# Norm boundaries of a two-part transformer stack: sums of squares in four column parts of TensorE, first products passed in another order

## The reference, cut to what matters

```python
x = x + gate * y
h = rms_norm(x, g) * (1 + scale) + shift
... h @ W ...

def _rmsnorm(x, g, eps=RMS_EPS):
    x32 = x.astype(jnp.float32)
    y = x32 * lax.rsqrt(jnp.mean(x32 * x32, axis=-1, keepdims=True) + eps)
    return (y * g.astype(jnp.float32)).astype(x.dtype)
```

## The kernel before

| boundary, start of Ln (us) | what follows | ahead | ada |
|---|---|---|---|
| 561.0, 1653.5 | MLP | two units | no |
| 927.2 | dilated attention, behind a barrier of all engines | no | 48 sums |
| 2019.6 | recurrent mixer | four quarters | 48 sums |
| 2752.7, 3343.0 | convolutional FFN | two units | no |
| 3135.0 | Fourier and convolution mixer | two units | 16 sums |
| 3722.7 | transposes and output | no | no |

## Time and profile before

### The profile page before, as it was taken

One profiled execution on the slowest core, in us unless ns is written; L12 is line 12 of the kernel. 1 busy time (PEld: TensorE's weight loads), 2 busy tenths in 40 slices (PEclk: granted clock), 3 DMA queues, 4 the chain that ended last, 5 costly groups with the idle time before them and its releaser, 6 DMA issues. The chain is left out here.

```text
span 3739.8 us, 62013 instructions
## 1 busy us (share of the span) xinstructions
PE 3428.5 (92%) x25014; PEld 2625.2 (70%) x25014; DVE 1960.2 (52%) x2407; ACT 1283.4 (34%) x2213; POOL 1168.0 (31%) x626
## 2 busy tenths in 40 slices
PE   6899989999899999789999997788699999989998
PEld 4445567888676777568888886666578877668876
DVE  8345536565355343556565573444357554853444
ACT  3245522223445455321223433332132223142222
POOL 0000024443565554134443322000035443124443
PEclk9899989999899999799999998788799999989999
DMA  6222214443343434225453211000035443113332
GB/s 243 82 79 68 65 62 173 158 169 112 113 133 113 128 112 110 93 78 186 152 175 98 76 54 40 4 4 4 25 124 185 140 161 99 56 62 96 95 95 79
DMA packets 261706, 383.85 MB, mean 103 GB/s; under 512 B 40406, under 2 KB 185466, under 8 KB 250234
## 3 DMA queue, kind: packets, MB, share of 16 engines
q1 hardware_dynamic: 257144, 366.90, 30.7%
q10 hardware_dynamic: 4354, 13.98, 0.9%
HBM read 360.90 MB, written 19.92 MB: 102 GB/s over the span
## 5 line engine op out<-in xcount | busy, mean ns | idle before, releaser
L487 POOL TENSOR_TENSOR w_lo<-w_raw,w_hi 128x1024 fp32r<-128x1024 f32 x302 | 750.4, 2485 | 1831.8 <-ACT w_hi L478 1831.8
L500 PE MATMUL ps<-h_hi,w_hi 128*128 128x512 f32 x2432 | 958.7, 394 | 66.9 <-DVE h_lo L684 33.2
L501 PE MATMUL ps<-h_hi,w_lo 128*128 128x512 f32 x2432 | 954.8, 393 | 0.0
L502 PE MATMUL ps<-h_lo,w_hi 128*128 128x512 f32 x2432 | 953.9, 392 | 0.0
L478 ACT ACTIVATE w_hi<-w_raw 128x1024 fp32r<-128x1024 f32 x302 | 320.3, 1061 | 1182.9 <-PE ps L502 1154.2
L500 PEld LDWEIGHTS ps<-h_hi,w_hi 128*128 128x128 f32 x2432 | 462.1, 190 | 179.2 <-issue 36.9
L502 PEld LDWEIGHTS ps<-h_lo,w_hi 128*128 128x128 f32 x2432 | 461.6, 190 | 97.1
L501 PEld LDWEIGHTS ps<-h_hi,w_lo 128*128 128x128 f32 x2432 | 462.0, 190 | 95.3
L792 DVE TENSOR_TENSOR h_lo<-big,h_hi 128x512 fp32r<-128x512 f32 x100 | 243.1, 2431 | 228.2 <-ACT h_hi L478 228.1
L1521 POOL TENSOR_TENSOR w_lo<-w_raw,w_hi 128x512 fp32r<-128x512 f32 x192 | 249.0, 1306 | 266.0 <-ACT w_hi L1702 261.8
L615 DVE SCALAR_TENSOR_TENSOR big<-yT,cond,big 128x2048 f32<-128x2048 f32 x63 | 178.7, 2837 | 91.3 <-DMA yT<-in_ada_w 91.0
(11 more groups left out here) (434 smaller groups left out, 5480.8 us busy)
## 6 DMA issues: line engine op xcount, KB each, us to landing
w_raw<-in_mlp_w SPq DMA_DIRECT2D x128, 512.0 KB, 3.7
yT<-in_ada_w SPq DMA_DIRECT2D x56, 1024.0 KB, 6.0
w_raw<-in_dil_w_in SPq DMA_DIRECT2D x192, 256.0 KB, 3.1
w_raw<-in_ffn_w_up SPq DMA_DIRECT2D x176, 256.0 KB, 3.0
h_free<-in_ada_w SPq DMA_DIRECT2D x24, 1024.0 KB, 5.0
w_raw<-in_ffn_w_down SPq DMA_DIRECT2D x44, 512.0 KB, 3.5
w_raw<-in_ab_w_in SPq DMA_DIRECT2D x70, 256.0 KB, 2.9
yT<-in_ada_w SPq DMA_DIRECT2D x32, 512.0 KB, 6.2
```

The costliest lines, as they stand in the source:

```text
L487: self.nc.gpsimd.tensor_tensor(self.w_lo[:, s, :], self.w_raw[:, s, :], self.w_hi[:, s, :].bitcast(F32), ALU.subtract).then_inc(sg["w_spli ...
L500: self.nc.tensor.matmul(out, w_hi, h_hi, start=start, stop=False)
L501: self.nc.tensor.matmul(out, w_lo, h_hi, start=False, stop=False)
L502: return self.nc.tensor.matmul(out, w_hi, h_lo, start=False, stop=stop)
```

## The change

Three things are changed.

1. In `norm_after` the eight products of the squares use only 32 columns of the ones, and k goes to the part k % 4: output partitions 32q to 32q + 31. After them a part holds the sum of two of the squares' tiles, the same in its 32 partitions. DVE copies the bank into yT tile 0 (its squares are no longer needed), and PE multiplies this by the full ones into the next bank, so that each total stands 32 times; Ln's scale becomes 1/(32 D). Two semaphores are added, parts and parts_in.
2. The second weight unit is rounded by ACT behind h_hi of k = 1 and no longer ahead of all h_hi. In `recurrent` the quarters 1, 2 and 3 are rounded behind h_hi of k = 0, 1 and 2.
3. The first unit's 24 passes are issued in another order (`first_unit`): for k = 0 the eight passes that read h_hi, which wait for `shifted` (h_hi of that k) alone, then the four that read h_lo, then the same for k = 1. In `recurrent`, `tokens(k)` does so for every k. All that is computed stays the same but for the order of additions.

```diff
+    def hi_passes(self, out, s, lo, h, start):
+
+        w_hi, w_lo, h_hi = self.w_hi[:, s, lo:lo + P], self.w_lo[:, s, lo:lo + P], self.h_hi[:, h, :]
         self.nc.tensor.matmul(out, w_hi, h_hi, start=start, stop=False)
         self.nc.tensor.matmul(out, w_lo, h_hi, start=False, stop=False)
-        return self.nc.tensor.matmul(out, w_hi, h_lo, start=False, stop=stop)
+
+    def lo_pass(self, out, s, lo, h, stop):
+        return self.nc.tensor.matmul(out, self.w_hi[:, s, lo:lo + P], self.h_lo[:, h, :], start=False, stop=stop)
...
+    def first_unit(self, pe, out, freed):
+
+        sg = self.sg
+        for k in range(2):
+            pe.wait_ge(sg["shifted"], sg.at("shifted", k + 1 - KT))
+            for b in range(TURN):
+                if k == 0:
+                    pe.wait_ge(sg["out_free"], sg.at("out_free", freed(b)))
+                self.hi_passes(out(b), 0, k * TURN * P + b * P, k, k == 0)
+            pe.wait_ge(sg["h_split"], sg.at("h_split", k + 1))
+            for b in range(TURN):
+                last = self.lo_pass(out(b), 0, k * TURN * P + b * P, k, False)
+        last.then_inc(sg["unit_done"], 1)
@@ stream_products (fourier_conv alike)
             for u in range(UNITS):
+                pe.wait_ge(sg["w_split"], sg.at("w_split", i * UNITS + (u + 1 + 2)))
+                if normed and u == 0:
+                    self.first_unit(pe, lambda b: self.ps[:, z * TURN + b, :], lambda b: i * TURN + b + 1)
+                    continue
                 if normed:
                     pe.wait_ge(sg["h_split"], sg.at("h_split", 2 * u + 2))
-                pe.wait_ge(sg["w_split"], sg.at("w_split", i * UNITS + (u + 1 + 2)))
@@ norm_after
-            nc.scalar.activation(self.rs[:], self.ps[:, bank, :], ACT.Ln, scale=1.0 / D, bias=self.eps[:, 0:1])
+            nc.scalar.activation(self.rs[:], self.ps[:, (bank + 1) % KT, :], ACT.Ln, scale=1.0 / (32 * D), bias=self.eps[:, 0:1])
...
-            if ahead is not None:
-                ahead[1](act)
             if layer is not None:
                 for k in range(KT):
                     act.wait_ge(sg["normed"], sg.at("normed", k + 1))
                     nc.scalar.activation(self.h_hi[:, k, :] if split else dst[:, k, :], dst[:, k, :], ACT.Identity,
                                          bias=shift(k)).then_inc(sg["shifted"], 1)
+                    if ahead is not None and k in ahead[1]:
+                        ahead[1][k](act)
...
                 pe.wait_ge(sg["squares"], sg.at("squares", k + 1))
-                last = nc.tensor.matmul(self.ps[:, bank, :], self.c["ones"][:], self.yT[:, k, :],
-                                        start=(k == 0), stop=(k == KT - 1))
-            last.then_inc(sg["sums"], 1)
+                q = slice(32 * (k % 4), 32 * (k % 4) + 32)
+                last = nc.tensor.matmul(self.ps[q, bank, :], self.c["ones"][:, 0:32], self.yT[:, k, :],
+                                        start=k < 4, stop=k >= 4)
+            last.then_inc(sg["parts"], 1)
+            pe.wait_ge(sg["parts_in"], sg.at("parts_in", 1))
+            nc.tensor.matmul(self.ps[:, (bank + 1) % KT, :], self.c["ones"][:], self.yT[:, 0, :],
+                             start=True, stop=True).then_inc(sg["sums"], 1)
...
         def _(v):
+            v.wait_ge(sg["parts"], sg.at("parts", 1))
+            nc.vector.tensor_copy(self.yT[:, 0, :], self.ps[:, bank, :]).then_inc(sg["parts_in"], 1)
@@ recurrent, tokens
-                pe.wait_ge(sg["h_split"], sg.at("h_split", k + 1))
+                pe.wait_ge(sg["shifted"], sg.at("shifted", k + 1 - KT))
...
                     nc.tensor.matmul(out, self.h_hi[:, k, t], w_hi, start=k == 0, stop=False)
-                    nc.tensor.matmul(out, self.h_lo[:, k, t], w_hi, start=False, stop=False)
-                    last = nc.tensor.matmul(out, self.h_hi[:, k, t], w_lo, start=False, stop=k == KT - 1)
+                    nc.tensor.matmul(out, self.h_hi[:, k, t], w_lo, start=False, stop=False)
+                pe.wait_ge(sg["h_split"], sg.at("h_split", k + 1))
+                for b in range(TT):
+                    last = nc.tensor.matmul(self.ps[:, 2 + b, :], self.h_lo[:, k, b * P:(b + 1) * P], w_hi, start=False,
+                                            stop=k == KT - 1)
```

More of the change, by code:

```diff
@@ L624, in first_units @@
     def first_units(self, parts=1):
-        return [lambda act, n=n: self.round_unit(act, self.act_copy, n, 1, n, parts) for n in range(2)]
+        unit = [lambda act, n=n: self.round_unit(act, self.act_copy, n, 1, n, parts) for n in range(2)]
+        return unit[0], {1: unit[1]}
     def norm_after(self, block, g, layer, sub, bank, split, ada=None, ahead=None, ada_later=False):
@@ L697, in _ @@
                 self.ada_bias(ada, (bank + KT - 2) % KT, 16, 48)
-        sg.passed(squares=KT, sums=1, rstd=1, normed=KT, shifted=0 if layer is None else KT, out_free=KT)
+        sg.passed(squares=KT, parts=1, parts_in=1, sums=1, rstd=1, normed=KT, shifted=0 if layer is None else KT, out_free=KT)
         if ada is not None:
@@ L2276, in _ @@
                 for u in range(UNITS):
+                    pe.wait_ge(sg["w_split"], sg.at("w_split", i * UNITS + u + 1 + 2))
+                    if i == 0 and u == 0:
+                        self.first_unit(pe, lambda b: self.ps[:, HOME[0] + b, :], lambda b: KT)
+                        continue
                     if i == 0:
                         pe.wait_ge(sg["h_split"], sg.at("h_split", 2 * u + 2))
-                    pe.wait_ge(sg["w_split"], sg.at("w_split", i * UNITS + u + 1 + 2))
                     for b in range(TURN):
@@ L2438, in first_quarters @@
     def first_quarters(self):
-        def rest(act):
-            for n in range(1, 4):
-                self.round_quarter(act, n)
-        return [lambda act: self.round_quarter(act, 0), rest]
+        quarter = [lambda act, n=n: self.round_quarter(act, n) for n in range(4)]
+        return quarter[0], {0: quarter[1], 1: quarter[2], 2: quarter[3]}
     def recurrent(self, block):
```

6 lines of the change are left out of this document (3 added, 3 removed).

## The result

The change took 3714.47 us in the median of 4 runs (3710.93 to 3724.88), beside 3747.84 for the kernel before (3743.28 to 3750.87, 4 runs). The ratio is 0.9917, with a 95% interval of 0.9894 to 0.9939: 31 us faster, between 23 and 40 (the two medians themselves lie 33 us apart). Run again later, it gave 3720.07 (6 runs) beside 3747.5 (29 runs), 0.9929 [0.9914, 0.9944], 27 us. The forecast was 23 us faster, 3725.5, range 3713 to 3742.

What follows compares the result with a forecast made beforehand. PE was taken as the bound, busy 92%, with gains in its waits at the eight norm boundaries. 11 + 8 + 0 + 0 + 1.8 + 2.3 = 23 us off 3748.5 gave 3725.5 us, range 3713 to 3742.

Steps and rivals of the forecast that it cites:

- DVE is not held up: Rival: POOL's w_lo finds a gap, PE's own passes set the third unit; 31.5 us won, 3717; chance 0.10.
- The sums, 2.3 us per boundary: Ones products at the norm boundaries: four column parts run at once, so Ln starts 2.3 us earlier.
- Only two parts: Rival for the ones products: only two column parts run at once; 9.6 us less won, 3735; chance 0.08.
- one behind another: Rival for the ones products: column parts run serially; 12 us slower than before, 3760; chance 0.07.
- The first product: First boundary: PE's first product waits only for an h_hi and starts at 561.8 instead of 568.2.
- DVE held up at its fourth L719: First boundary: POOL's w_lo of the second unit blocks DVE's fourth h_lo operation, which ends 0.55 us after w_lo.
- The third unit is next the late one: Weight-unit boundaries: PE waits for the third unit's w_lo; at an MLP it starts at 576.3 instead of 581.8.
- The clock takes the gain: Rival: PE stays at half clock through the first two units, nothing won at five boundaries; about 3750; chance 0.12.
- 11 us for the MLPs: Two MLP boundaries: the third unit starts 5.5 us earlier at each, 11 us in all.
- 8 us for the FFNs: Two FFN boundaries, with ACT's table load between: the third unit starts 4.0 us earlier at each, 8 us in all.
- 1.8 us for the Fourier mixer: Boundary at 3135 us, where the norm waits for 32 adaLN records: 1.8 us won, between 0.2 and 3.3.
- 0 for the two boundaries with 48 adaLN sums: Boundaries at 927 and 2020 us: between 2.3 us won and 2.5 lost by the clock, the middle, 0, was taken.

Runs made afterwards that it cites:

- One part: The change with all eight 32-column ones products in one and the same column part: 3763.34 us (1 run), beside 3741.18 for the kernel before.
- before with six drains: The kernel before with six drains added to DVE's program ahead of its tap loop: 3754.54 us (1 run), beside 3747.13 for the kernel before.
- the change with ten: The change with ten drains added to DVE's program ahead of its tap loop: 3710.33 us (6 runs), ratio 0.9928 to the kernel before.

## Why the prediction was right, and where not

The range 3713 to 3742 and the mechanism held. Both medians, 3714.47 and 3720.07, lie in its lower part, the first outside the narrower 3720 to 3731 that the forecast gave itself, and both some 3 us from the 3717 of *DVE is not held up*, a rival that the trace refutes. So the total alone does not decide for the forecast; the single steps do. Point by point:

- **The sums, 2.3 us per boundary.** Measured 2.40 (Ln at 5.45 and 3.05 us), at all eight. The steps hold too: parts done at 1.1 behind the square, the copy of 0.69 at 1.14, the ninth product at 1.88, 0.05 behind the copy and not 0.25. The change of the products' width, for which the forecast had under 0.2 us from rows and added nothing to its sum, doesn't show: the full-width product stands 0.05 us behind the copy. But PE had been idle for 0.79 us there, so no run here shows what it costs a busy PE. Four parts overlap fully, which was taken from two column parts and four row parts. *Only two parts* and *one behind another* are false. "One part" shows the price of the latter: Ln 4.4 us later than in the change, as the rival had it, and 6 to 11 us more than before in the quiet stretches, 22 in one measured total (the rival: 12).
- **The first product** starts at 6.29 and started at 12.68, 6.39 earlier; 6.4 was forecast.
- **DVE held up at its fourth L719**: 2.88 us. *DVE is not held up* is false. L719 starts 0.34 us behind POOL's w_lo (569.04), ends 0.55 us behind it, and takes 2.88 us where the operation behind it takes 0.74. So it is at the first boundary in all fourteen traces: one operation of DVE, of 2.62 to 2.88 us, stands beside w_lo of the second unit and ends 0.54 to 0.55 us behind it. By what the two exclude each other was not shown.
- **The third unit is next the late one**: 5.8 and 5.7 us earlier at the MLPs (forecast 5.5), 4.2 and 4.3 at the FFNs (forecast 4.0), 2.9 at the Fourier mixer (forecast 1.8, up to 3.3). Between the second traces it is 4.8, 5.7, 3.2, 4.3 and 3.1: the change repeats to 0.13 us there, and the kernel before was 1.0 us earlier at the first MLP and the first FFN, with less time at half clock. PE waited for POOL at all of them, 0.3 to 3.1 us, 1.61 at the first. At the Fourier mixer DVE started the norm 8.03 us behind the square and 10.50 before, 2.5 earlier; the forecast's bounds were 7.4 and 10.5. The 32 records of L604 took 4.65 us, between the 3.5 and 6.7 of its two clocks.
- **The clock takes the gain**: false. It rose 2.8 to 6.0 us into the products, so the 48 passes were done before the third unit was there. The forecast's own working has a slip here: 561.8 + 5.5 is 567.3 and not 569.7, which lies outside its 3 to 7 us as well (the trace of before shows 2.9 to 5.5 at its seven boundaries with products behind). With 567.3 the second unit ends at the 575.1 that it gives; with 569.7 it would end at 576.4, and PE would not wait at all. Measured, the last of the 48 passes starts 18.4 to 19.9 us behind the square; the 575.1, an end, is 19.5 behind it.
- **11 us for the MLPs**: 6.26 + 6.17 = 12.4 between the first traces, and 10.1 between the second. The forecast lies between. The 0.5 us more than at the third unit in the first pair were lost by the kernel before behind that unit; in its second trace it did not lose them.
- **8 us for the FFNs**: this is the first term that was mis-sized. The third unit came earlier as forecast, but "behind this point PE is bound by its own passes, so the gain stays" fails there. The stretches got 2.9 and 3.1 us shorter, 6.0 in all (4.1 between the second traces: 1.1 and 3.0). In the second FFN PE's start is 4.15 us earlier at every product from the 60th to the 1020th. Then, 255 us behind the square (259 before), two products start 2.24 us apart in both kernels, and behind that pause the clock fell in the change alone, in both pairs of traces. Busy time by stretch, 3.4 us from 0.7 us behind the pause, the change and then before:

```profile
3584.50:3587.90 3.40, 3.08 (x8) 2.21 (x8) 1.25 (x2) 1.10 (x2) 0.00 (x0) 0.50 0.28 112
```

```profile
3599.70:3603.10 3.40, 3.00 (x13) 2.03 (x12) 1.31 (x3) 1.58 (x2) 0.58 (x1) 1.00 0.29 116
```

  1.1 us were gone there. The first FFN lost 1.7 at its start: PE sat idle for 3.05 us before the third unit, and behind it the clock was at 0.50 for another 3.4 us. In the second trace of the change this didn't happen (idle 1.58 us, clock at 1.00), and the lead was lost later, 1.2 us of it at the same pause. The two rows of the first trace:

```profile
2760.96 0.50 PE L499 MATMUL ps<-h_hi,w_hi 128*128 128x512 f32 x1 [3.05 <-POOL w_lo L487]
```

```profile
2761.90:2765.30 3.40, 3.40 (x10) 2.65 (x9) 3.28 (x2) 0.00 (x0) 1.34 (x1) 0.50 0.98 360
```

- **1.8 us for the Fourier mixer**: measured 0.0. The step before the third unit won 2.9, DVE's loop gave back 3.1. That is the second mis-sized term, and no row of before could show it. With the short round the stretch won 2.4.
- **The last boundary, 2.3 us**: 2.47.
- **0 for the two boundaries with 48 adaLN sums**: the first product behind them starts at 31.6 and 20.3 us behind the square, and started at 30.6 and 21.0: one later, one earlier, as a zero would have it. (In the second traces 29.4 and 20.3 against 31.1 and 20.5.) The last of the 96 records ends at 22.0 and 20.4, and ended at 21.0 and 21.1, within the 2 us that the forecast allowed. But the stretches behind are two of the noisy ones. From either trace of before to either of the change, the one is from 1.3 us longer to 6.9 shorter, the other from 1.0 longer to 15.2 shorter. All traces with the same code in these stretches say a little more: seven with the change's code average 722.8 in the one, against 725.3 in three of before; in the other it is 734.6 in five against 740.7 in three. They scatter by 8 and 13 us, so that the change wins something there is a hint and not shown.

The quiet stretches give 20.9 or 16.6 us against 23 forecast. The measured 27 and 31 are more. What lies between, 6 to 14 us, would have to come from the noisy stretches, where the traces can't tell it from the variation of one program. The intervals of the totals, 21 to 32 and 23 to 40 us, have the 20.9 at their lower edge or outside. So that the forecast's 23 stands between the two measures is partly luck: its terms for the FFNs and the Fourier mixer were 2 to 4 and 1.8 us too high, and the two zeros may be too low.

Of the three edits the sums give 13 us, and the order and the rounding together the other 13. With the new order in place the later rounding gives nothing: the quiet sum of the change is 2.1 us above that of the kernel without it. The order alone would therefore have done.

## What to carry to other kernels

When a wait of the bottleneck engine is shortened, look for the next late one and price the gain by it: here the third unit's w_lo held the boundaries to 3 to 6 us, although PE itself started 6.4 us earlier at the MLPs and FFNs, and the load of the fifth was the next. When two edits are made for the same wait, undo each by itself and both together: one of them may be doing nothing. The sums over partitions by a matrix of ones got by with 32 of its columns here: four parts at once, one copy and one product more beat eight full products by 2.4 us, since only what is left behind the last square counts. And where the time of a kernel moves by 10 us from run to run, cut the traces at fixed events, compare the stretches, and take two traces of each kernel.

## What the runs showed of the hardware that was not expected

- A loop of DVE with the same instructions and the same waits takes 0.12 us more or less per round, by where it stands in the engine's program: 6.9 or 10.0 us of idle time in 25 rounds. Six more instructions ahead of it make it slow (the change, and before with six drains), sixteen don't (the change with ten). The cause was not shown.
- Four 32-column products with all 128 rows, each with its own moving operand of 512 fp32 elements, run fully at once, into one PSUM bank. The passes of the four parts start within 0.02 us, and the next four 0.43 to 0.45 us later.
- The same code ahead of the first boundary took 553 to 561 us in the executions traced, with 65 to 85 us of it at clock 0.50.
